# Three of eight stick-breaking heads summed in full fp32 instead of as high and low fp32r parts

## The chip, the cores and the metric

The kernel runs on one core of one Trainium2 chip. The metric is the device time of one execution in microseconds (us); lower is better. Engines are named as the profile names them: PE is TensorE, PEld its weight loads, DVE is VectorE, ACT is ScalarE, POOL is GpSimd, SP is SyncE, which issues most of the DMAs.

## The reference

One layer of a hybrid decoder runs over 512 prompt tokens and 32 sample tokens: a half-step feed-forward block, a mixing block, a second half-step feed-forward block and a per-layer embedding. The mixing block has a gated linear attention (GLA) group of 4 heads and a stick-breaking group of 8 heads. Only the second group is touched here:

```
def sb_attend(q, k, v, q_pos, k_pos, bias):
    z = einsum(q, k) * SB_DH ** -0.5 + bias
    valid = k_pos < q_pos
    log_stay = where(valid, log_sigmoid(-z), 0)
    after = cumsum(log_stay, reverse=True) - log_stay     # over the keys
    w = where(valid, exp(log_sigmoid(z) + after), 0)
    return einsum(w, v)
```

`log_sigmoid(-z)` is minus the softplus of z. So each head needs, for each query, running sums of a softplus over the later keys. All inputs and outputs are fp32.

## The kernel before

Activations are held transposed, features on the 128 partitions and 544 tokens along the row. The large matmuls (feed-forward blocks, projections) are made from three fp32r products, high times high, low times high and high times low; DVE and ACT make the high and low parts. They run before and after the part that matters here.

The stick-breaking heads of the prompt run in a loop over h = 0 to 7. The causal part of a 512x512 score matrix, keys on partitions, is held as 1280 columns: 4 diagonal blocks of 128 (columns 0 to 511), then the blocks right of the diagonal, 384 + 256 + 128 columns. For each head:

1. PE makes the scores of a pair of heads in units (`z_unit`, lines 1014, 1019 and, for the cached pages of the samples, 1030); ACT copies them out with the bias (`logits`, L1619).
2. ACT makes exp and log (`soft_part`, L1629 and L1631), DVE finishes the softplus (`softplus`, L2434) in `sb_s[h % 3]` and signals `sp_ready`.
3. DVE rounds the softplus to fp32r (`high`, L2441 and L2442) and subtracts that from it (`low`, L2447), both parts in fp32r; it signals `sp_low_ready`.
4. PE sums over the keys (`prompt_sums`, L1093): matmuls with a triangular mask within a block and a matrix of ones for whole blocks. There are nine products of 512, 384, 384, 256, 128, 384, 256, 128 and 128 columns, 2560 in all. Each is made twice, of the high and of the low part, so there are 18 matmuls. They go to PSUM banks 4 to 6, of which there is one set, so `prompt_sums(h)` waits for `d_ready` of head h-1.
5. DVE subtracts the sums from the scores (`exponents`, L2454 and L2455) and signals `d_ready`; ACT takes the exponential (`weight`, L1686) and signals `w_ready`.
6. PE multiplies with the values after every second head (`prompt_out`, L1124 and L1126); DVE copies the result out (`pair_out`, L2461).

The order on each engine is written out by hand. PE runs `prompt_sums(h)`, then `prompt_out` of the pair before (h = 2, 4, 6), then the score units that `Z_STEP[h]` names. After h = 5 comes `sample_z` (L1158), after h = 6 `head_sum(0)` and `head_sum(1)` (L1147, sums of squares of the GLA heads, whose squares ACT makes at L1695), and after h = 7 the sample's sums with the full fp32 masks (`sample_sums`, L1168 to L1172), `head_sum` and `prompt_out(3)`. DVE runs for each h: `low(h + 1)`, `exponents(h)`, `softplus(h + 2)`, `high(h + 2)`, and after some heads `pair_out` and copies of the values (L2430).

Of the kernel before, what the change touches and what calls it, by code (L numbers as in the profile page):

```python
# [33 lines left out]
SB_HEADS, SB_DH = 8, 64  # L34
# [83 lines left out]
def build(nc, a, o):  # L118
# [13 lines left out]
    with ctx:  # L132
        def sb(name, shape, dt=F32, where=ctx):
            return where.enter_context(nc.sbuf_tensor(name, shape, dt))

        def sem(name):
            return ctx.enter_context(nc.semaphore(name))

        PS = ctx.enter_context(nc.psum_tensor("PS", [P, 8, 512], F32))
# [9 lines left out]
        ones = sb("ones", [P, P])  # L149
        tri = sb("tri", [P, P])  # L150
# [52 lines left out]
        def scratch(owner, at_, shape):  # L203

            n = 1
            for s_ in shape[1:]:
                n *= s_
            v = owner[0:shape[0], at_:at_ + n]
            if len(shape) == 3:
                return v.rearrange("p (a b) -> p a b", a=shape[1])  # L210
            if len(shape) == 4:
                return v.rearrange("p (a b c) -> p a b c", a=shape[1], b=shape[2])
            return v
# [6 lines left out]
        p_raw = scratch(extra_flat, 8 * HALF, [P, 2, T])  # L220

        spare = [hold_w[:, n, (at["out"][0] + 1) % 2, :] for n in range(2)]
        first_slot, other_slot = at["out"][0] % 2, (at["out"][0] + 1) % 2
        sb_z = [scratch(extra_flat, 0, [P, 1280]), raw[:, first_slot, 0:1280], scratch(spare[0], 0, [P, 1280]),
                scratch(extra_flat, 2560, [P, 1280]), scratch(dead, 2560, [P, 1280]), raw[:, other_slot, 0:1280],
# [2 lines left out]
        sb_s = [scratch(gone, 0, [P, 1280]), scratch(extra_flat, 1280, [P, 1280]), scratch(spare[1], 0, [P, 1280])]  # L228
# [12 lines left out]
        Z_UNITS = [(0, 1, None), (0, 0, None), (0, 2, None), (1, 0, None), (1, 1, None), (1, 2, (0, 0)), (2, 0, None),  # L241
                   (2, 1, (0, 1)), (2, 2, None), (3, 0, None), (3, 1, (1, 0)), (3, 2, (1, 1))]
        Z_FIRST = 5
        TURN = len(Z_UNITS)
        Z_STEP = [(5, 7), (7, 9), (9, 10), (10, 12), (12, 13), (13, 13), (13, 13), (13, 13)]
        PAGE_UNIT = {r: n for n, (p, u, r) in enumerate(Z_UNITS) if r is not None}
# [91 lines left out]
        sig = {n: sem(n) for n in names}  # L338
# [222 lines left out]
        def _(pe):  # L561
            mm = nc.tensor.matmul
# [418 lines left out]
            def z_unit(n):  # L981

                banks_ = unit_banks(n)
                if n in (0, 1, 3):

                    t = T0["rest"] + REST - (3, 2, None, 1)[n]
                    pe.wait_ge(psum_free[t % 2], t // 2 + 1)
                elif n == 4:
                    pe.wait_ge(sig["og_out"], GLA_HEADS)
                    pe.wait_ge(sig["sn_out"], 8)  # L990
                else:
                    pe.wait_ge(sig["z_out"], n if n in (2, TURN) else n - 1)
                if n == TURN:
                    last = pages_turned(banks_[0])
                else:
                    p, u, r = Z_UNITS[n]
                    last = prompt_z(p, u, banks_)
                    if r is not None:
                        last = page_z(*r, banks_[0])
                last.then_inc(sig["z_full"], 1)  # L1000
# [34 lines left out]
            def pages_turned(bank):  # L1035

                for n in range(4):
                    cols_ = slice(n * P, (n + 1) * P)
                    last = nc.tensor.transpose(PS[:, bank, cols_], z_past[:, cols_], ident[:])
                return last  # L1040
# [28 lines left out]
            def natural(r):  # L1069
# [11 lines left out]
                                               flat(proj[:, SV + f])[:, r * P:(r + 1) * P], ident[:])  # L1081
                last.then_inc(sig["nat_full"], 1)

            def prompt_sums(h):

                parts = [sp_low[h % 3][:, a_:b_] for a_, b_ in ((0, 512), (512, 1280))]
                pe.wait_ge(sig["sp_low_ready"], h + 1)
                pe.wait_ge(sig["d_ready"], h)

                def both(out, mask, at_, n, start=False, stop=False):  # L1090
                    for i, (diag, rest) in enumerate((sp_high[h % 2], parts)):
                        src = diag[:, at_:at_ + n] if at_ < 512 else rest[:, at_ - 512:at_ - 512 + n]
                        last = mm(out, mask, src, start=start and i == 0, stop=stop and i == 1)  # L1093
                    return last

                both(PS[:, 4, :], tri_r, 0, 512, start=True, stop=True)
                both(PS[:, 5, 0:384], tri_r, 512, 384, start=True)
                both(PS[:, 5, 0:384], ones_r, 128, 384)
                both(PS[:, 5, 128:384], ones_r, 896, 256)
                both(PS[:, 5, 256:384], ones_r, 1152, 128, stop=True)  # L1100
                if h == 0:
                    pe.wait_ge(sig["nat_out"], 1)
                both(PS[:, 6, 0:384], tri_r, 896, 384, start=True)
                both(PS[:, 6, 0:256], ones_r, 256, 256)
                both(PS[:, 6, 128:256], ones_r, 1152, 128)
                both(PS[:, 6, 256:384], ones_r, 384, 128, stop=True).then_inc(sig["c_full"], 1)
# [46 lines left out]
            def sample_z():  # L1153

                pe.wait_ge(sig["setup_new"], 2)
                pe.wait_ge(sig["z_out"], TURN)
                for p in range(4):
# [16 lines left out]
            for quad in range(2):  # L1174
                pe.wait_ge(psum_free[quad], (T0["merge"] + 1 - quad) // 2)
            for n in range(3, Z_FIRST):
                z_unit(n)
            natural(0)
            for h in range(SB_HEADS):
                prompt_sums(h)  # L1180
                if h == 7:
                    head_sum(2)
                    sample_sums()
                    head_sum(3)
                    prompt_out(3)
                elif h % 2 == 0 and h:
                    prompt_out(h // 2 - 1)
                if h == 6:
                    head_sum(0)
                    head_sum(1)  # L1190
                if h == 1:
                    natural(3)
                for n in range(*Z_STEP[h]):
                    z_unit(n)
                    if n < Z_FIRST + 2:
                        natural(n - Z_FIRST + 1)
                if h == 5:
                    sample_z()
# [93 lines left out]
        def _(act):  # L1292
# [387 lines left out]
            soft_part(1)  # L1680
            for n in range(3, Z_FIRST + 1):
                logits(n)
# [41 lines left out]
            for h in range(SB_HEADS):  # L1724
# [11 lines left out]
                for n in range(*Z_STEP[h]):  # L1736
                    if Z_FIRST < n < TURN:
                        logits(n)
# [127 lines left out]
        def _(dve):  # L1866
# [569 lines left out]
            def high(n):  # L2436
                dve.wait_ge(sig["sp_ready"], n + 1)
                if n >= 2:
                    dve.wait_ge(sig["c_full"], n - 1)
                s_ = sb_s[n % 3]  # L2440
                v.tensor_copy(sp_high[n % 2][0], s_[:, 0:512])  # L2441
                v.tensor_copy(sp_high[n % 2][1], s_[:, 512:1280]).then_inc(sig["sp_high_ready"], 1)  # L2442

            def low(n):
                dve.wait_ge(sig["sp_high_ready"], n + 1)
                for high_, first, end in zip(sp_high[n % 2], (0, 512), (512, 1280)):
                    ins = v.tensor_tensor(sp_low[n % 3][:, first:end], sb_s[n % 3][:, first:end], high_.bitcast(F32),  # L2447
                                          ALU.subtract)
                ins.then_inc(sig["sp_low_ready"], 1)
# [17 lines left out]
            def sample_logits():  # L2467

                dve.wait_ge(sig["setup_new"], 2)
                dve.wait_ge(sig["z_full"], TURN + 1)  # L2470
                v.scalar_tensor_tensor(z_past.rearrange("p (a n) -> p a n", a=2),
                                       PS[:, unit_banks(TURN)[0], :].rearrange("p (a n) -> p a n", a=2), SB_DH ** -0.5,
                                       cols.unsqueeze(1).broadcast_to([P, 2, 256]), ALU.mult,
# [21 lines left out]
            softplus(1, sb_z[1], sb_s[1])  # L2495
            high(1)
            for h in range(SB_HEADS):
                if h + 1 < SB_HEADS:
                    low(h + 1)
                exponents(h)  # L2500
                if h == 0:
                    natural_out(1)
                    natural_out(2)
                elif h == 1:
                    natural_out(3)
                if h + 2 < SB_HEADS:
                    softplus(h + 2, sb_z[h + 2], sb_s[(h + 2) % 3])
                    high(h + 2)
                if h == 5:
                    sample_logits()  # L2510
                elif h == 6:
                    softplus(SB_HEADS, z_past, s_past)
                    softplus(SB_HEADS + 1, z_new, s_new)
                if h % 2 == 0 and h:
                    pair_out(h // 2 - 1)
                if h == 6:
                    out_low(0)
# [63 lines left out]
            n, t, quad, use = F_TILES, *ticket(Step(0), "f2_up0")  # L2581
# [346 lines left out]
```

## Time and profile before

| | |
|---|---|
| median of 3 runs | 1181.87 us (1181.6 to 1182.53) |
| the profiled execution | 1181.77 us, span 1179.6 us |
| PE busy | 1159.6 us, 98% of the span |
| DVE busy | 778.2 us, 66% |
| ACT busy | 547.9 us, 46% |
| granted PE clock | 1.00 |

The profiled execution has a span (first to last instruction) of 1179.6 us; 2.2 us lie around it. The loop over the heads is about 49 us of it, from 602.1 to 651.3 us. PE is almost always busy over the whole span, so the few microseconds where it waits are what other engines can give back. A "duration" in a timeline holds the pipeline's fill and drain: an engine starts the next instruction before the end of the last, and the step from start to start is what a stream of instructions costs.

### The profile page before, as it was taken

Reading aid. Unit: us, or ns where it says so; the run is one execution under the profiler, and the core shown is the slowest. Engines: PE = TensorE matmul, PEld = TensorE weight load, DVE = VectorE, ACT = ScalarE, POOL = GpSimd, SP = SyncE. Lnnn points to the kernel's source line nnn. Section 1 sums busy time; section 2 is a strip of 40 time slices with the busy share of each in tenths; the row PEclk is TensorE's granted clock in tenths of the full one; section 3 lists DMA queues with packets and bytes.
Section 4 is the critical chain, followed back from the end, with each engine's and each line's share of the span. In section 5 each row is a group of like instructions: output and inputs, shape, how many; then the busy total and the mean of one; then the engine's idle time right before and its main releaser. Section 6 shows DMA issues by size and latency. Waiting matters only on the chain.

```text
span 1179.6 us, 23057 instructions
## 1 busy us (share of the span) xinstructions
PE 1159.6 (98%) x9230; PEld 1119.7 (95%) x9230; DVE 778.2 (66%) x1075; ACT 547.9 (46%) x758; POOL 105.3 (9%) x138
## 2 busy tenths in 40 slices
PE   7999999999999999999999999999999999999997
PEld 6999999999999999999877699999999999999996
DVE  6853887368845865655379747863788358864665
ACT  5433555235543532312368745533555225544555
POOL 1600000000002012122050010000000000002102
PEclk9999999999999999999999999999999999999999
DMA  6203331232224032213047151113421233215202
GB/s 220 86 28 124 121 107 54 90 124 93 87 72 148 17 108 73 70 59 113 1 150 241 59 179 37 38 58 93 143 86 68 90 125 107 89 54 179 72 1 77
DMA packets 45405, 110.29 MB, mean 93 GB/s; under 512 B 5458, under 2 KB 11618, under 8 KB 45202
## 3 DMA queue, kind: packets, MB, share of 16 engines
q1 hardware_dynamic: 43522, 103.13, 26.0%
q0 software_dynamic: 1232, 5.01, 1.3%
q8 instruction: 55, 0.90, 0.3%
q10 hardware_dynamic: 576, 1.08, 0.2%
q14 instruction: 20, 0.16, 0.0%
HBM read 103.57 MB, written 5.64 MB: 93 GB/s over the span
## 4 chain that ended last, share of the span: by engine, by line
PE 92%; DVE 4%; ACT 2%; DMA 1%; issue 0%; SPq 0%; DVEq 0%; ACTq 0%
PE PS L584 42%; PE PS L795 29%; PE PS L597 12%; PE PS L915 1%; PE PS L765 1%; DMA raw<-in_f_in 1%; PE PS L618 1%; PE PS L942 1%; PE PS L975 1%; PE PS L978 0%; PE PS L1019 0%; DVE extra L2434 0%; SPq L517 0%; PE PS L1147 0%; DVE w_lo L1874 0%
## 5 line engine op out<-in xcount | busy, mean ns | idle before, releaser
L1300 ACT ACTIVATE w_hi<-raw 128x1024 fp32r<-128x1024 f32 (+2 forms) x77 | 93.2, 1210 | 155.4 <-PE PS L584 128.4
L1874 DVE TENSOR_TENSOR w_lo<-raw,w_hi 128x1024 fp32r<-128x1024 f32 (+2 forms) x76 | 108.1, 1422 | 79.2 <-ACT w_hi L1300 79.2
L795 PE MATMUL PS<-a_lo,w_hi 128*128 128x272 f32 x512 | 148.7, 290 | 0.0
L584 PE MATMUL PS<-a_hi,w_hi 128*128 128x272 f32 x656 | 139.6, 294 | 8.9 <-DVE w_lo L2175 7.6
L795 PE MATMUL PS<-a_hi,w_lo 128*128 128x272 f32 x512 | 147.6, 288 | 0.0
L795 PE MATMUL PS<-a_hi,w_hi 128*128 128x272 f32 x512 | 147.4, 288 | 0.0
L584 PE MATMUL PS<-a_lo,w_hi 128*128 128x272 f32 x656 | 136.3, 289 | 0.0
L584 PE MATMUL PS<-a_hi,w_lo 128*128 128x272 f32 x656 | 136.0, 289 | 0.0
L584 PE MATMUL PS<-h_hi,w_hi 128*128 128x272 f32 x576 | 119.5, 289 | 0.2
L584 PE MATMUL PS<-h_hi,w_lo 128*128 128x272 f32 x576 | 119.2, 288 | 0.0
L584 PE MATMUL PS<-h_lo,w_hi 128*128 128x272 f32 x576 | 118.8, 288 | 0.0
L584 PEld LDWEIGHTS PS<-a_hi,w_hi 128*128 128x128 f32 x656 | 103.2, 189 | 13.5 <-issue 10.7
L584 PEld LDWEIGHTS PS<-a_lo,w_hi 128*128 128x128 f32 x656 | 103.8, 190 | 0.0
L584 PEld LDWEIGHTS PS<-a_hi,w_lo 128*128 128x128 f32 x656 | 103.5, 190 | 0.0
L795 PE MATMUL PS<-b_tail,w_hi 128*128 128x272 f32 x512 | 98.0, 289 | 0.0
L795 PEld LDWEIGHTS PS<-a_hi,w_hi 128*128 128x128 f32 x512 | 96.6, 189 | 0.0
L795 PEld LDWEIGHTS PS<-a_hi,w_lo 128*128 128x128 f32 x512 | 96.4, 188 | 0.0
L795 PEld LDWEIGHTS PS<-a_lo,w_hi 128*128 128x128 f32 x512 | 96.1, 188 | 0.0
L584 PEld LDWEIGHTS PS<-h_hi,w_hi 128*128 128x128 f32 x576 | 90.5, 188 | 0.8 <-DVE h_lo L1995 0.6
L584 PEld LDWEIGHTS PS<-h_lo,w_hi 128*128 128x128 f32 x576 | 90.5, 189 | 0.0
L584 PEld LDWEIGHTS PS<-h_hi,w_lo 128*128 128x128 f32 x576 | 89.9, 189 | 0.0
L795 PEld LDWEIGHTS PS<-b_tail,w_hi 128*128 128x128 f32 x512 | 80.3, 188 | 0.0
(471 smaller groups left out, 2615.6 us busy)
## 6 DMA issues: line engine op xcount, KB each, us to landing
raw<-in_f_in SPq DMA_DIRECT2D x86, 512.0 KB, 4.0
raw<-in_f_out SPq DMA_DIRECT2D x64, 256.0 KB, 2.8
raw<-in_w_rest SPq DMA_DIRECT2D x40, 256.0 KB, 2.8
raw<-in_f_out SPq DMA_DIRECT2D x32, 192.0 KB, 2.4
raw<-in_w_out SPq DMA_DIRECT2D x8, 512.0 KB, 5.0
raw<-in_ple_w_gate SPq DMA_DIRECT2D x8, 512.0 KB, 4.2
x<-in_x SPq DMA_DIRECT2D x8, 272.0 KB, 7.2
raw<-in_w_in SPq DMA_DIRECT2D x4, 512.0 KB, 4.0
```

What stands on the lines that cost most here:

```text
L584: last = mm(PS[0:width, 4 * quad + 2 * c + half, 0:HALF], wt[:, cols], act[:, k, half * HALF:(half + 1) * HALF], start=(k == 0 and n == 0) ...
L597: last = mm(PS[0:width, 4 * quad + 2 * c + half, 0:HALF], wt[:, cols], act[:, k, tok], start=(k == 0 and n == 0), stop=(k == n_k - 1 and n ...
L618: last = mm(PS[:, 4 * quad + 2 + half, 0:HALF], ones[:], squares[:, tok], start=(k < summed), stop=(k == KD - 1))
L765: last = mm(PS[:, 4 * (t % 2) + 2 * c + half, 0:HALF], wt[:, slot, col:col + P], act[:, k, half * HALF:(half + 1) * HALF], start=(k == 0 a ...
L795: last = mm(PS[:, 4 * quad + bank, 0:HALF], w_[:, k * P:(k + 1) * P], a_[:, k, :], start=(start and k == 0 and i == 0), stop=(stop and k = ...
L915: last = mm(PS[:, 2 + hh, tok], k_[r, tok], q_[r, tok], start=True, stop=True)
L942: last = mm(PS[:, 7, n * 256:n * 256 + 256], kl_batch[:, 2 * part + n, :], gv_new[:, p * 256:(p + 1) * 256], start=True, stop=True)
L975: last = mm(PS[:, 2 + hh, tok], gv_nat[:, c, h * P:(h + 1) * P], att[p][:, N_CH * hh + c, :], start=True, stop=(c == 0))
L1300: fn(pair[0][:, 0:width], raw[:, slot, 0:width], ACT.Copy).then_inc(sig["split_hi"], 1)
L1874: v.tensor_tensor(pair[1][:, 0:width], raw[:, slot, 0:width], pair[0][:, 0:width].bitcast(F32), ALU.subtract).then_inc(sig["split_lo"], 1)
```

## The change

A tuple `PLAIN_SUMS = (2, 4, 6)` names the third, fifth and seventh head. For these PE uses `plain_sums`: nine matmuls of fp32 operands, the softplus itself against the fp32 masks `tri` and `ones`, where `prompt_sums` had 18 of fp32r parts. It waits for `sp_ready` instead of `sp_low_ready`. DVE leaves out `high` and `low` for these heads. `split_heads(n)` counts the heads before n that are still split, for the waits on the semaphores of the two parts. Buffers, banks, the masks and the order of everything else stay.

```diff
+        def split_heads(n):
+
+            return n - sum(h < n for h in PLAIN_SUMS)
...
+        PLAIN_SUMS = (2, 4, 6)
...
+            def plain_sums(h):
+
+                s_ = sb_s[h % 3]
+                pe.wait_ge(sig["sp_ready"], h + 1)
+                pe.wait_ge(sig["d_ready"], h)
+                mm(PS[:, 4, :], tri[:], s_[:, 0:512], start=True, stop=True)
+                mm(PS[:, 5, 0:384], tri[:], s_[:, 512:896], start=True, stop=False)
+                mm(PS[:, 5, 0:384], ones[:], s_[:, 128:512], start=False, stop=False)
+                mm(PS[:, 5, 128:384], ones[:], s_[:, 896:1152], start=False, stop=False)
+                mm(PS[:, 5, 256:384], ones[:], s_[:, 1152:1280], start=False, stop=True)
+                mm(PS[:, 6, 0:384], tri[:], s_[:, 896:1280], start=True, stop=False)
+                mm(PS[:, 6, 0:256], ones[:], s_[:, 256:512], start=False, stop=False)
+                mm(PS[:, 6, 128:256], ones[:], s_[:, 1152:1280], start=False, stop=False)
+                mm(PS[:, 6, 256:384], ones[:], s_[:, 384:512], start=False, stop=True).then_inc(sig["c_full"], 1)
+
             def prompt_sums(h):
...
-                pe.wait_ge(sig["sp_low_ready"], h + 1)
+                pe.wait_ge(sig["sp_low_ready"], split_heads(h) + 1)
...
-                prompt_sums(h)
+                (plain_sums if h in PLAIN_SUMS else prompt_sums)(h)
...
             def low(n):
-                dve.wait_ge(sig["sp_high_ready"], n + 1)
+                dve.wait_ge(sig["sp_high_ready"], split_heads(n) + 1)
...
-                if h + 1 < SB_HEADS:
+                if h + 1 < SB_HEADS and h + 1 not in PLAIN_SUMS:
                     low(h + 1)
...
-                    high(h + 2)
+                    if h + 2 not in PLAIN_SUMS:
+                        high(h + 2)
```

PE before, from the end of the score unit ahead of the third head's sums (`proj` holds q and k, `work_r` and `h_hi` the high part, `w_lo` the low part, `sum_r` the masks in fp32r):

```order
L1019 MATMUL PS<-proj 128x256
L1019 MATMUL PS<-proj 128x128 x2
L1093 MATMUL PS<-work_r,sum_r 128x512 [waits d_ready,sp_low_ready]
L1093 MATMUL PS<-w_lo,sum_r 128x512
L1093 MATMUL PS<-h_hi,sum_r 128x384
L1093 MATMUL PS<-w_lo,sum_r 128x384
L1093 MATMUL PS<-work_r,sum_r 128x384
L1093 MATMUL PS<-w_lo,sum_r 128x384
```

PE in the changed kernel, at the same place (`hold_w` is the softplus of the third head):

```order
L1025 MATMUL PS<-proj 128x256
L1025 MATMUL PS<-proj 128x128 x2
L1095 MATMUL PS<-hold_w,tri 128x512 [waits d_ready,sp_ready]
L1096 MATMUL PS<-hold_w,tri 128x384
L1097 MATMUL PS<-hold_w,ones 128x384
L1098 MATMUL PS<-hold_w,ones 128x256
L1099 MATMUL PS<-hold_w,ones 128x128
L1100 MATMUL PS<-hold_w,tri 128x384
L1101 MATMUL PS<-hold_w,ones 128x256
L1102 MATMUL PS<-hold_w,ones 128x128
L1103 MATMUL PS<-hold_w,ones 128x128
```

Nine rows stand where 18 stood. In this listing a matmul of full fp32 is one row; the trace records it as two matmuls.

DVE before, from the third head's softplus to the fourth's (`hold_w` and `proj` are the softplus buffers, `raw` the scores of the second head):

```order
L2434 SCALAR_TENSOR_TENSOR hold_w<-hold_w 128x1280 [waits soft_log]
L2441 CAST work_r<-hold_w 128x512 [waits c_full,sp_ready]
L2442 CAST h_hi<-hold_w 128x768
L2447 TENSOR_TENSOR w_lo<-hold_w,work_r 128x512 [waits sp_high_ready]
L2447 TENSOR_TENSOR w_lo<-hold_w,h_hi 128x768
L2454 TENSOR_TENSOR raw<-raw,PS 128x512 [waits c_full]
L2455 TENSOR_TENSOR raw<-raw,PS 128x768
L2430 COPY v_nat<-PS 128x512 [waits nat_full]
L2434 SCALAR_TENSOR_TENSOR proj<-proj,extra 128x1280 [waits soft_log]
```

DVE in the changed kernel, the same stretch:

```order
L2455 SCALAR_TENSOR_TENSOR hold_w<-hold_w 128x1280 [waits soft_log]
L2475 TENSOR_TENSOR raw<-raw,PS 128x512 [waits c_full]
L2476 TENSOR_TENSOR raw<-raw,PS 128x768
L2451 COPY v_nat<-PS 128x512 [waits nat_full]
L2455 SCALAR_TENSOR_TENSOR proj<-proj,extra 128x1280 [waits soft_log]
```

Four instructions are gone from between the softplus of the third head and the exponents of the second. The same holds one and two pairs of heads later.

## Rows read from the trace of the kernel before

**Rows 1.** The page: one engine's busy time, and the chain by engine.
```profile
PE 1159.6 (98%) x9230; PEld 1119.7 (95%) x9230; DVE 778.2 (66%) x1075; ACT 547.9 (46%) x758; POOL 105.3 (9%) x138
PE 92%; DVE 4%; ACT 2%; DMA 1%; issue 0%; SPq 0%; DVEq 0%; ACTq 0%
```

**Rows 2.** Stretch: length, busy (instructions) of PE, PEld, DVE, ACT, POOL; clock, DMA.
```profile
602.10:651.27 49.17, 45.76 (x459) 38.40 (x458) 45.79 (x63) 41.03 (x55) 7.34 (x13) 1.00 0.61 205
```

**Rows 3.** PE's waits, 602 to 1180 us: total, times, longest.
```profile
PE PS L1093 <- DVE raw L2455: 1.8, 2, 1.3
PE PS L618 <- ACT sq L1360: 1.0, 1, 1.0
PE PS L1080 <- DVE v_nat L2430: 0.9, 1, 0.9
PE PS L1147 <- ACT hold_w L1695: 0.7, 1, 0.7
```

**Rows 4.** Chain of waits, in order of time: start, us, what.
```profile
619.63 1.56 DVE h_hi L2447 x2
...
648.82 2.61 PE PS L1093 x18
```

**Rows 5.** PE's timeline at the third head: start, duration, instruction, idle before.
```profile
615.41 0.92 PE L1019 MATMUL PS<-proj 64*128 64x256 f32 x8
616.81 0.47 PE L1093 MATMUL PS<-work_r,sum_r 128*128 128x512 f32 x1 [0.48 <-DVE raw L2455]
617.12 0.40 PE L1093 MATMUL PS<-w_lo,sum_r 128*128 128x512 f32 x1
...
619.58 0.32 PE L1126 MATMUL PS<-extra,v_nat 128*64 128x128 f32 x1
```

**Rows 6.** PE's timeline, fifth to seventh head: start of sums, what follows them.
```profile
630.19 0.50 PE L1093 MATMUL PS<-work_r,sum_r 128*128 128x512 f32 x1
...
632.99 0.32 PE L1126 MATMUL PS<-hold_w,v_nat 128*64 128x128 f32 x1
...
638.51 1.07 PE L1158 MATMUL PS<-sq,proj 128*32 128x64 f32 x8
640.88 0.47 PE L1093 MATMUL PS<-work_r,sum_r 128*128 128x512 f32 x1 [1.29 <-DVE raw L2455]
...
643.65 0.32 PE L1126 MATMUL PS<-proj,v_nat 128*64 128x128 f32 x1
```

**Rows 7.** PE's timeline where it already multiplies full fp32.
```profile
609.90 0.65 PE L1080 MATMUL PS<-ident,proj 128*128 128x128 f32 x4 [0.93 <-DVE v_nat L2430]
610.31 0.48 PE L1093 MATMUL PS<-work_r,sum_r 128*128 128x512 f32 x1
...
651.27 1.13 PE L1147 MATMUL PS<-hold_w,ones 128*128 128x272 f32 x4
652.24 1.02 PE L1168 MATMUL PS<-extra,tri 128*128 128x512 f32 x2
653.10 0.59 PE L1169 MATMUL PS<-extra,ones 128*128 128x256 f32 x2
653.62 0.69 PE L1170 MATMUL PS<-extra,ones 32*128 32x256 f32 x2
```

**Rows 8.** DVE's timeline: high part, low part and exponents; exponents of the fifth head.
```profile
612.71 0.43 DVE L2441 CAST work_r<-hold_w 128x512 fp32r<-128x512 f32 x1
...
613.64 0.69 DVE L2447 TENSOR_TENSOR w_lo<-hold_w,work_r 128x512 fp32r<-128x512 f32 x1
...
615.12 0.68 DVE L2454 TENSOR_TENSOR raw<-raw,PS 128x512 f32<-128x512 f32 x1
615.72 0.95 DVE L2455 TENSOR_TENSOR raw<-raw,PS 128x768 f32<-128x768 f32 x1
...
633.10 0.69 DVE L2454 TENSOR_TENSOR proj<-proj,PS 128x512 f32<-128x512 f32 x1 [0.56 <-PE PS L1093]
```

**Rows 9.** ACT's timeline: squares of the first two GLA heads.
```profile
645.97 1.19 ACT L1695 ACTIVATE hold_w<-y 128x544 f32<-128x544 f32 x2
```

## The prediction

> **What bounds the kernel now.** I read the page first. PE is busy for 98% of the span and makes 92% of the chain that ended last [rows 1], so a microsecond more of PE work is a microsecond of time unless PE was waiting there. Then the busy time of each engine in the stretch that the change touches, from the first head's sums to the end of the last one's: of 49.17 us PE is busy 45.76 and DVE 45.79, at a granted clock of 1.00 [rows 2]. Neither is far ahead. The chain of waits shows how they share it: for most of the stretch it runs through DVE (high part, low part, exponents, one after the other), and from about 647 us through PE alone [rows 4]. Read alone, this chain would say that DVE is the bound and that relieving it pays in full. PE's own waits say how much that can be worth: in the stretch it waits 1.8 us in two places for DVE's exponents, 0.9 us for a copy of the values and 0.7 us for ACT's squares [rows 3]. These 3.4 us are all that any relief of the other engines can give back there (49.17 - 45.76). None of PE's waits from 602 us on is put down to a DMA; the one behind the stretch that is over 0.7 us, 1.0 us at L618, is for ACT, on work that itself follows PE [rows 3]. So a shift of PE at the end of the heads should go through to the end of the kernel.
>
> **What the change takes from DVE.** The high part takes 0.93 us (612.71 to 613.64) and the low part 1.48 us (613.64 to 615.12) [rows 8], 2.4 us a head and 7.2 us for three heads. That is a sixth of DVE's 45.79 us in the stretch [rows 2], but it lies beside PE's work except where PE waits. DVE's own order also gets shorter between a softplus and the exponents behind it, so the exponents start when the sums are there.
>
> **What it takes from and adds to PE.** The split sums last from 616.81 to 619.58 us in the third head [rows 5], from 630.19 to 632.99 in the fifth and from 640.88 to 643.65 in the seventh [rows 6]: 2.77, 2.80 and 2.77, together 8.34 us. Within them a 128x512 matmul and the first of its partner stand 0.31 us apart [rows 5].
>
> The plain sums are not in the trace, but the same form is: right behind the heads the samples' sums use the fp32 mask `tri`, and their 512 columns are recorded as two matmuls which take 0.86 us, from 652.24 to 653.10 [rows 7]. That is 0.84 ns for a column of one record, 1.68 ns for a column of an fp32 matmul. Narrower ones don't seem to pay a floor: four recorded passes of 128 columns take 0.41 us (609.90 to 610.31), which is 0.80 ns a column, and four of 272 take 0.97 us, or 0.89 ns [rows 7]. So the 2560 columns of a head cost 2560 x 1.68 = 4.30 us. An edge is added: the two records of 256 columns in front of a matmul of other rows take 0.52 us, 0.09 over the rate [rows 7], and behind a head stands such a change too. I take 4.4 us a head, 13.2 us for three. The ends: 4.2 us (the transposes' two times 0.80 ns throughout, 4.1, and the edge) and 5.2 us (the 0.52 us of 256 columns, 2.03 ns a column, throughout). I stay by the row of 512 columns, since it has the same mask, the same operand types and a full set of 128 rows, and the 0.52 us has its edge in it.
>
> PE's work grows by 13.2 - 8.34 = 4.86 us.
>
> On passes the Trainium skill ("FP8 and Floating Point Precision", TensorE Precision Notes) says that true fp32 takes four passes through the array, for the products of high and low halves. Counting passes alone, four stand where two stood, and the sums would double, to 5.56 us a head. The rows say less than double: 0.86 us for 512 columns [rows 7] against 0.31 us for the first of the two split matmuls [rows 5], and for narrow ones hardly more than the pair. What that count would give is a rival below.
>
> **What PE's waits give back.** They are taken one by one.
> - Ahead of the third head PE waits 0.48 us for the second head's exponents [rows 5], which DVE starts at 615.12 [rows 8] only because high and low of the third head stand before them. Without these they start at about 613.2, when the second head's sums end, and are done by 614.8; the score unit ends at 615.41 + 0.92 = 616.33 [rows 5]. All 0.48 us come back.
> - Ahead of the seventh head's sums PE waits 1.29 us for the sixth head's exponents [rows 6]. Here the loop cannot be shorter than exponents behind sums: DVE starts 0.11 us after PE's next operation (633.10 against 632.99) [rows 6, 8], the two subtractions take 1.55 us (615.12 to 616.67) [rows 8], and PE starts 0.14 us later (616.81) [rows 5], 1.80 us in all against 2.37 now (638.51 to 640.88) [rows 6]. So 0.57 us come back, and 0.7 us of waiting stay, which is the wait that takes the place of the old one.
> - Ahead of `head_sum(0)` PE waits 0.7 us for ACT's squares [rows 3], which start at 645.97 [rows 9]. PE comes there about 3.8 us later than now (4.86 - 0.48 - 0.57), and ACT, which follows the sixth exponents, the sample's scores and their softplus, about 3 us later, by 649.0 against PE's 649.8. So 0.71 us come back, with a margin of 0.8.
> - The 0.93 us ahead of the transposes of L1080 [rows 7] lie before the first changed instruction and wait on DVE work that stays. Nothing comes back.
>
> The plain sums of heads 2, 4 and 6 are early enough otherwise: `sp_ready` comes before what `sp_low_ready` needed. The sums of heads 3, 5 and 7 wait for the exponents of a plain head, which now end later; PE has prompt_out and score units between (2 us or more), DVE needs 1.8. Sums: 0.48 + 0.57 + 0.71 = 1.76 us.
>
> **The sum.** +4.86 - 1.76 = +3.10 us on the profiled execution's 1181.77 us is 1184.87; it lies 0.10 under the median of 1181.87, so for a median I say 1185.0 us. A measurement of this kernel tells 0.2%, 2.36 us, from no change, so the line to slower is 1184.2.
>
> **The rivals.**
> - *No change that can be told (under +2.36 us).* The plain sums cost 4.2 us a head: 12.6 - 8.34 - 1.76 = +2.5, and a few tenths more come back, such as the dearer start of the split sums after other matmuls (0.31 against 0.23 us of a 128x512, three times 0.08, [rows 5]). That gives +2.2, 1184.1 us. For it: the narrow passes of L1080. Against: it needs both. Chance 0.17.
> - *Faster: DVE is the bound.* The chain does run through it [rows 4]. If a plain sum cost no more than a split one (the pair of narrow matmuls does cost about what one plain would), 1.76 us would come back and nothing be paid: 1180.1 us. It decides from the point where three plain heads take less than 8.34 + 1.76 = 10.1 us, 3.4 us each. The samples' 0.86 us for 512 columns [rows 7] speak against it. Chance 0.04.
> - *Four passes against two.* 3 x 2.78 = 8.3 us more, less 1.76: +6.6, 1188.5 us. The row of 0.86 us speaks against. Chance 0.04.
> - *Relief hidden anyway.* PE's waits don't shrink because ACT, not DVE, is behind them (softplus of the seventh head, the squares): up to the whole 4.86, 1186.7 us, likelier +3.9 with the squares' 0.7 lost. Chance 0.08.
>
> The forecast keeps 0.67. **Chances:** faster 0.04; same 0.18; slower 0.78, from the forecast, the last two rivals and less a little for its lower edge. The range reaches from 1184.0, into the second case, to 1186.4, where plain heads of 4.85 us end (14.55 - 8.34 - 1.76 = +4.5). The bound of 5.2 us a head (+5.5, 1187.4) and the four passes are left out, with the faster case, as the two in ten.
>
> **What would show it.** In the changed profile, L1095 to L1103 should have 54 matmul records and last about 4.4 us from the first start to the next operation. DVE's busy time in the stretch should be 7 us or so lower and idle time should stand before the exponents, released by PE. PE should have no wait ahead of the third head's sums, 0.7 us ahead of the seventh's, none before L1147 at 650 us. From the last head's sums on, all should be as before, 3.1 us later. The prediction is wrong if a plain head takes under 4.1 or over 4.8 us, if PE shows a new wait for `exponents` ahead of heads 3, 5 or 7, or if the delay at 650 us isn't found again at the end.

## The result

The changed kernel takes 1184.92 us in the median (1182.05 before, in the same rounds), a ratio of 1.0025, 95% interval 1.0018 to 1.0031: 2.1 to 3.7 us slower. Of 18 executions of each kernel one was far off (1213.43 us in the changed kernel, 1613.86 us before); it counts in the median and not in the ratio. The forecast was 1185.0 us. That this is within 0.1 us of the median is partly luck: the difference of the medians is 2.87 us where the forecast had 3.1, and it was added to an earlier median of before (1181.87) that lay 0.18 lower.

The page gives the profiled execution a span of 1183.3 us (1185.45 us with what lies around it); its engine line answers to [rows 1]:

```profile
PE 1165.1 (98%) x9230; PEld 1121.7 (95%) x9230; DVE 772.5 (65%) x1063; ACT 548.6 (46%) x758; POOL 104.1 (9%) x138
```

PE has the same number of records and 5.5 us more to do, DVE 12 instructions and 5.7 us less. The stretch from the first head's sums to the end of the last head's, and from PE's first output matmul (674.22; the window opens 0.02 us ahead of it) to the end, by engine as in [rows 2]:

```profile
602.53:655.02 52.49, 50.83 (x460) 39.54 (x458) 38.88 (x51) 41.73 (x56) 7.33 (x13) 1.00 0.58 192
...
674.20:1183.30 509.10, 501.43 (x3918) 496.42 (x3918) 333.67 (x455) 246.12 (x350) 28.64 (x20) 1.00 0.26 87
```

Before, the same two stretches were 49.17 us [rows 2] and, from the answer to the same view, this:

```profile
670.47:1179.60 509.13, 501.50 (x3918) 496.49 (x3918) 333.90 (x455) 245.86 (x350) 28.62 (x20) 1.00 0.26 87
```

So 3.32 us come in within the stretch, and nothing is made up behind it: its second line is 509.10 us (509.08 from the matmul itself) against 509.13. In the stretch PE is busy 5.07 us longer (50.83 - 45.76) and idle 1.66 us where it had been idle 3.41. DVE is busy 6.9 us less and has nothing to show for it: PE went on setting the pace. The two spans differ by 3.7 us; the rest is 0.43 us ahead of the first head's sums (602.53 against 602.10), where nothing was changed, less the 0.05 behind; in the other profiles of this study that point lies between 601.64 and 602.74, so it belongs to no change.

PE's timeline from the end of the score unit to the products behind the third head's sums, columns as in [rows 5]:

```profile
615.84 0.92 PE L1025 MATMUL PS<-proj 64*128 64x256 f32 x8
616.69 1.12 PE L1095 MATMUL PS<-hold_w,tri 128*128 128x512 f32 x2
617.65 0.81 PE L1096 MATMUL PS<-hold_w,tri 128*128 128x384 f32 x2
618.30 0.81 PE L1097 MATMUL PS<-hold_w,ones 128*128 128x384 f32 x2
618.95 0.59 PE L1098 MATMUL PS<-hold_w,ones 128*128 128x256 f32 x2
619.38 0.38 PE L1099 MATMUL PS<-hold_w,ones 128*128 128x128 f32 x2
...
620.90 0.39 PE L1103 MATMUL PS<-hold_w,ones 128*128 128x128 f32 x2
621.21 0.32 PE L1147 MATMUL PS<-extra,v_nat 128*64 128x128 f32 x1
```

The wait of 0.48 us [rows 5] is gone. From start to start the matmuls of 384, 256 and 128 columns take 0.65, 0.43 and 0.22 us, all about 1.7 ns a column, as the 1.68 of 512 columns, with no floor down to 128. The first takes 0.96 us instead of 0.86 and the last 0.31 instead of 0.22. The head takes 4.52 us, and its nine rows are 18 records, as in the other two plain heads. The fifth takes the same (631.82 to 636.34) and the seventh 4.49:

```profile
641.85 1.07 PE L1179 MATMUL PS<-sq,proj 128*32 128x64 f32 x8
643.66 1.10 PE L1095 MATMUL PS<-proj,tri 128*128 128x512 f32 x2 [0.73 <-DVE raw L2476]
...
648.15 0.32 PE L1147 MATMUL PS<-proj,v_nat 128*64 128x128 f32 x1
...
650.47 2.10 PE L1168 MATMUL PS<-hold_w,ones 128*128 128x272 f32 x8
```

Ahead of the seventh head PE waits 0.73 us (1.29 before, [rows 6]), and none ahead of the squares' sums at 650.47 (0.7 before, [rows 3]). These two are all that is left of PE's waits in the stretch that the profile names, total, times and longest as in [rows 3]; the first lies ahead of the second head and is as it was:

```profile
PE PS L1086 <- DVE v_nat L2451: 0.9, 1, 0.9
PE PS L1095 <- DVE raw L2476: 0.7, 1, 0.7
```

DVE's side of it, its own waits in the stretch:

```profile
DVE extra L2475 <- PE PS L1114: 3.3, 1, 3.3
DVE proj L2475 <- PE PS L1103: 2.8, 1, 2.8
```

These are the two longest. The exponents wait for PE's sums in six of the eight heads now, where it had been two; the time taken from DVE has turned into idle time of DVE.

### The profile page after: what moved, and what is told of

It is laid out like the page before. It is cut to its first block, busy times and chain, and to the rows that moved or that the text cites. A ratio compares the mean times of both kernels' runs of the same rounds, so it can differ in the third digit from the quotient of the medians.

```text
span 1183.3 us, 23042 instructions
## 1 busy us (share of the span) xinstructions
PE 1165.1 (98%) x9230; PEld 1121.7 (95%) x9230; DVE 772.5 (65%) x1063; ACT 548.6 (46%) x758; POOL 104.1 (9%) x138
## 4 chain that ended last, share of the span: by engine, by line
PE 95%; DVE 2%; ACT 1%; issue 0%; DMA 0%; DVEq 0%; ACTq 0%
PE PS L590 43%; PE PS L801 29%; PE PS L603 11%; PE PS L921 1%; PE PS L771 1%; PE PS L1114 1%; PE PS L1025 1%; PE PS L624 1%; PE PS L948 1%; PE PS L981 0%; PE PS L1145 0%; PE PS L984 0%; DMA raw<-in_f_in 0%; PE PS L1168 0%; PE PS L1147 0%
```

## The experiments

Few of these differences can be told apart by the times alone: most intervals are about 1 us to either side. So each experiment is also read in its profile, which is a single execution, from the start of the first head's sums to the start of the first sum of squares (44.65 us before, 602.10 to 646.75; 47.94 in the changed kernel, 602.53 to 650.47).

| kernel | to the first sum of squares | against before | ratio, 95% interval |
|---|---|---|---|
| changed | 47.94 | +3.29 | 1.0025 (1.0018 to 1.0031) |
| e1_parts_kept | 48.80 | +4.15 | 1.0037 (1.0023 to 1.0050) |
| e2_relief_only | 43.58 | -1.07 | 0.9991 (0.9982 to 1.0000) |
| e3_only_seventh | 45.03 | +0.38 | 1.0005 (0.9996 to 1.0014) |
| e4_only_third | 45.63 | +0.98 | 1.0003 (0.9994 to 1.0012) |
| e5_only_fifth | 46.92 | +2.27 | 1.0009 (1.0000 to 1.0018) |
| e6_all_plain | 53.70 | +9.05 | 1.0082 (1.0068 to 1.0095) |
| v2_copy_squares | 43.45 | -1.20 | 0.9994 (0.9985 to 1.0003) |
| v3_squares_first | 45.38 | +0.73 | 0.9997 (0.9988 to 1.0006) |
| v4_copy_squares_pair | 42.99 | -1.66 | 0.9996 (0.9987 to 1.0005) |

**e1_parts_kept: PE's half of the change alone.**

```diff
-            return n - sum(h < n for h in PLAIN_SUMS)
+            return n
...
-                if h + 1 < SB_HEADS and h + 1 not in PLAIN_SUMS:
+                if h + 1 < SB_HEADS:
                     low(h + 1)
...
-                    if h + 2 not in PLAIN_SUMS:
-                        high(h + 2)
+                    high(h + 2)
...
-                    ins = v.tensor_tensor(sp_low[n % 3][:, first:end], sb_s[n % 3][:, first:end], high_.bitcast(F32),
-                                          ALU.subtract)
+                    ins = v.tensor_tensor(high_ if n in PLAIN_SUMS else sp_low[n % 3][:, first:end],
+                                          sb_s[n % 3][:, first:end], high_.bitcast(F32), ALU.subtract)
```

Expected:

> The changed kernel, but DVE still makes high and low part of the third, fifth and seventh head (the low part over the high one, since PE reads neither), 7.2 us of DVE work with no reader. Theory A (PE's plain sums cost 5.2 us, DVE's relief gives back 1.05 us through two waits of PE, and PE coming late covers ACT's squares for 0.7): against before +5.2 - 0.7 = +4.5 us, 1.05 over the changed kernel; PE waits about 0.5 us ahead of the third head's sums and 1.3 ahead of the seventh's, as before, none ahead of the squares' sums. Rival B (relief of DVE is worth nothing, PE's waits vanish because PE comes later): like the changed kernel, +3.3 us. Rival C (DVE's relief is worth its whole length): +3.3 + 7.2 = +10.5 us.

Measured: 1185.85 us, ratio 1.0037 (1.0023 to 1.0050). In its profile PE's waits in the stretch are these:

```profile
PE PS L1095 <- DVE raw L2477: 1.6, 2, 1.1
PE PS L1086 <- DVE v_nat L2451: 0.9, 1, 0.9
```

They are 0.48 us ahead of the third head, as before, and 1.07 ahead of the seventh; the wait for the squares is gone. That is +4.15 us against before and 0.86 over the changed kernel, where theory A had 4.5 and 1.05. The interval of the time, 2.7 to 5.9 us, excludes rival C (7.2 us of DVE work paid in full) but not rival B (+3.3); against B speak the two waits, which are back with DVE as their releaser while the plain sums stay. Of the 0.35 us by which A was off against before, 0.22 are the wait of 1.07 us instead of 1.29. Before, the seventh head's softplus starts on DVE 1.07 us behind the second subtraction ahead of it (633.71 to 634.78), right behind the end of ACT's log (633.48 + 1.27 = 634.75). Here PE, and DVE with it, come later, ACT's log ends at 635.88, and the same step takes 0.87 us (637.04 to 637.91).

**e2_relief_only: DVE's half alone.**

```diff
-                mm(PS[:, 4, :], tri[:], s_[:, 0:512], start=True, stop=True)
...
+                def twice(out, mask, at_, n, start=False, stop=False):
+                    diag, rest = sp_high[0]
+                    for i in range(2):
+                        src = diag[:, at_:at_ + n] if at_ < 512 else rest[:, at_ - 512:at_ - 512 + n]
+                        last = mm(out, mask, src, start=start and i == 0, stop=stop and i == 1)
+                    return last
+
+                twice(PS[:, 4, :], tri_r, 0, 512, start=True, stop=True)
...
```

Expected:

> The other half alone: DVE leaves out high and low part of the three heads and PE waits for the softplus alone, but makes the 18 matmuls of a split sum, in fp32r, reading the first head's high part twice, so the sums of these three heads are left wrong. Theory A: the three heads last 2.8 us each, the 0.48 us ahead of the third head and 0.57 of the 1.29 ahead of the seventh come back, the 0.7 us for ACT's squares stay, since ACT moves along with PE: -1.05 us against before. Rival B: no change. Rival C (the chain of waits through DVE taken at its word): -3 us or more, up to all of PE's 3.4 us of waits in the stretch.

Measured: 1180.48 us, ratio 0.9991 (0.9982 to 1.0000); in the profile -1.07 us, as theory A had it (-1.05). The interval of the time, -2.1 us to none, excludes rival C (-3 us or more) and just reaches rival B (no change); against B speaks the profile. PE's waits in the stretch:

```profile
PE PS L1086 <- DVE v_nat L2459: 0.9, 1, 0.9
PE PS L1100 <- DVE raw L2484: 0.7, 1, 0.7
PE PS L1176 <- ACT hold_w L1724: 0.7, 1, 0.7
```

The wait ahead of the third head is gone, that ahead of the seventh is down to 0.73 us, and the 0.7 us for the squares stay. The three heads' sums take 2.80, 2.81 and 2.76 us, within 0.03 us of before, so nothing else has changed on PE. So 7.2 us of DVE work less are worth 1.07 us to PE. The last of the three waits also settles that the squares' 0.7 us come back in the changed kernel through PE's lateness and not through DVE's relief.

**e3_only_seventh, e4_only_third, e5_only_fifth: one head at a time.**

```diff
-        PLAIN_SUMS = (2, 4, 6)
+        PLAIN_SUMS = (6,)        # e4: (2,)   e5: (4,)
```

Expected:

> Only the seventh head is plain. Theory A: +1.73 for PE's sums (4.5 against 2.77), -0.57 at the wait ahead of it, -0.7 at ACT's squares, which PE now reaches later: +0.45 us against before. If what comes back had nothing to do with the place, it would be a third of the joint change, +1.1 us.

> Only the third head is plain. Theory A: +1.73 us for PE's sums, -0.48 at the wait ahead of them, the later waits stay, since DVE and ACT still make the same work between the fifth head's sums and the seventh's: +1.25 us against before. By thirds of the joint change: +1.1 us.

> Only the fifth head is plain. Theory A: PE did not wait ahead of the fifth head, so DVE's relief there gives back nothing and the whole +1.73 us is paid. By thirds of the joint change: +1.1 us.

Measured, by time: 1181.76, 1182.15 and 1182.75 us, ratios 1.0005 (0.9996 to 1.0014), 1.0003 (0.9994 to 1.0012) and 1.0009 (1.0000 to 1.0018). None is told apart from thirds of the joint change (+1.1 us) by these intervals. The profiles do it: +0.38, +0.98 and +2.27 us. For the seventh head alone PE's waits are 0.9 ahead of the transposes, 0.5 ahead of the third head, 0.7 ahead of the seventh and none for the squares, as forecast, for +0.45. For the third alone they are these:

```profile
PE PS L1114 <- DVE raw L2476: 1.1, 1, 1.1
PE PS L1086 <- DVE v_nat L2451: 0.9, 1, 0.9
PE PS L1168 <- ACT hold_w L1716: 0.7, 1, 0.7
```

That is 0.48 us back ahead of the third head and 0.2 more than forecast ahead of the seventh (1.07 for 1.29, the wait for ACT again): 0.98 instead of 1.25. The fifth head alone comes out 0.5 us above its +1.73, for a reason of its own. The profiled execution is the slowest of e5's eleven (1184.36 us, against a median of 1182.75), and its timeline behind the wait shows why:

```profile
640.61 1.08 PE L1179 MATMUL PS<-sq,proj 128*32 128x64 f32 x8
642.76 0.47 PE L1114 MATMUL PS<-work_r,sum_r 128*128 128x512 f32 x1 [1.07 <-DVE raw L2476]
643.07 1.23 PE L1114 MATMUL PS<-h_hi,sum_r 128*128 128x512 f32 x3
...
647.09 0.32 PE L1147 MATMUL PS<-proj,v_nat 128*64 128x128 f32 x1
```

The seventh head's split sums take 4.33 us, not 2.77. By stretches of 1 us, columns as in [rows 2], with the granted clock third from the end:

```profile
642.00:643.00 1.00, 0.24 (x1) 0.27 (x2) 1.00 (x2) 0.35 (x1) 0.00 (x0) 1.00 1.05 293
643.00:644.00 1.00, 1.00 (x4) 0.85 (x4) 1.00 (x1) 1.00 (x2) 0.00 (x0) 0.55 0.83 268
644.00:645.00 1.00, 1.00 (x5) 1.00 (x5) 0.96 (x4) 1.00 (x1) 0.00 (x0) 0.50 0.86 301
...
647.00:648.00 1.00, 1.00 (x10) 0.58 (x11) 1.00 (x2) 0.97 (x4) 0.00 (x0) 1.00 0.00 0
```

The granted clock is 0.50, the 1.2 GHz level, for about 3.4 us, behind a microsecond in which PE was mostly idle. That costs 1.56 us here and hides the 0.7 us wait for the squares. Without it the sum would be 1.74 for the plain head less 0.22 at the seventh, +1.5 us, with the squares' wait still there. So e5's +2.27 us is no clean measure of the fifth head; its time, +1.1 us (0.0 to +2.1), agrees with this sum and with a third of the joint change alike.

**e6_all_plain: all eight heads.**

```diff
-        PLAIN_SUMS = (2, 4, 6)
+        PLAIN_SUMS = tuple(range(8))
...
-            high(0)
-            low(0)
             natural_out(0)
             softplus(1, sb_z[1], sb_s[1])
-            high(1)
```

`plain_sums` also has the first head's wait for `nat_out` ahead of bank 6, as `prompt_sums` has it.

Expected:

> All eight heads plain, DVE makes no high or low part in this stage. Theory A: 8 x 1.73 = +13.8 us, and all of PE's waits that can come back do, 0.93 + 0.48 + 0.57 + 0.71 = 2.7: +11.1 us against before. Rival B (nothing comes back by relief): +12.4 or more. Rival C (DVE is the bound and 19 us are taken from it): well under +10 us.

Measured: 1191.65 us, ratio 1.0082 (1.0068 to 1.0095), +8.0 to +11.2 us. In the profile +9.05 us to the first sum of squares with seven heads behind it, of which PE's sums make +11.8 (31.2 us against 19.4) and waits -2.7. At the first output matmul it is +10.84 us (681.25 - 602.04 = 79.21, against 68.37), where A had +11.1; the eighth head makes 1.5 of the 1.8 between. The time's upper end excludes rival B (+12.4 us or more); rival C (well under +10) is excluded by the profile alone. The wait of 0.9 us ahead of the transposes has gone too, the one of 0.7 ahead of the seventh head is the last:

```profile
602.04:670.00 67.96, 67.23 (x512) 46.06 (x510) 35.16 (x44) 47.79 (x66) 4.80 (x9) 1.00 0.43 144
```

PE is idle 0.7 us in 68, so in this stretch hardly anything is left to give back, whatever is taken from DVE.

This profile also shows what an edge of the plain sums depends on. The eighth head stands between matmuls of the same form, 128 rows by 128, on both sides:

```profile
657.68 1.02 PE L1095 MATMUL PS<-extra,tri 128*128 128x512 f32 x2
...
662.00 1.08 PE L1170 MATMUL PS<-hold_w,ones 128*128 128x272 f32 x4
```

It takes 4.32 us, the bare rate of 1.68 ns for 2560 columns, and so does the second (4.33), between transposes of that form. The first and the sixth, which have it on one side alone, take 4.42, and the third, fourth and fifth, which have matmuls of fewer rows or columns on both sides, 4.52 or 4.53.

**v2_copy_squares, v3_squares_first, v4_copy_squares_pair: the waits without the plain sums.** The three waits that the change shortened can be attacked by order alone.

```diff
                 if h + 1 < SB_HEADS:
                     low(h + 1)
+                if h == 0:
+                    natural_out(1)
                 exponents(h)
+                if h == 5:              # v4 only
+                    pair_out(1)
                 if h == 0:
-                    natural_out(1)
                     natural_out(2)
...
-                if h % 2 == 0 and h:    # v4 only
+                if h in (2, 6):         # v4 only
                     pair_out(h // 2 - 1)
...
                     log_part(SB_HEADS + 1, z_new, s_new)
+                if h == 5:
                     act.wait_ge(sig["o_full"], 2)
                     head_square(0)
                     head_square(1)
                 weight(h, sb_z[h])
...
                     pe.wait_ge(sig["zs_out"], 1)
+                elif i == 1:
+                    pe.wait_ge(sig["zs_out"], 2)
```

v3 has the last two parts alone, and all are made from the kernel before. Expected:

> The kernel before with two changes of order and nothing plain: DVE copies the second block of values before the first head's exponents, not after, and ACT squares the first two GLA heads before the sixth head's weights, not after the samples' logarithms (PE's second sum of squares then waits for the samples' scores itself). Theory A, that only PE's waits count here: the 0.9 us ahead of the transposes shrink by 0.3 to 0.5, DVE's chain gets 0.45 us shorter, and the 0.7 us ahead of the sums of squares go: -1.2 us against before. If the chain of waits is made up elsewhere: 0 to -0.5 us.

> The kernel before with the squares of the first two GLA heads moved ahead of the sixth head's weights on ACT, alone. Theory A: the 0.7 us ahead of the sums of squares go, 0.7 us less than before. If ACT's other work pays for it (the sixth head's weights start 1.1 us later): the weights are needed only 3 us later by PE, so nothing; should it be otherwise, 0.

> The two changes of order of v2_copy_squares, and DVE copies out the second pair's result after the sixth head's exponents and not ahead of the sixth head's end (0.6 us off DVE's way between the fifth and the sixth exponents). No head is plain. Theory A: the 1.29 us ahead of the seventh head's sums become 0.73, as they did where DVE left out the seventh head's parts; with the 0.8 us that the trace of v2_copy_squares showed at the end of the heads this makes -1.4 us against before. If the wait ahead of the seventh head isn't DVE's length but PE's: -0.8 us, as v2_copy_squares. Where the granted clock of PE falls behind that wait in some executions, a shorter wait should make this rarer, which could take up to 0.5 us more off the median.

Measured: 1181.28, 1181.14 and 1180.81 us, against medians of the kernel before of 1181.61, 1181.64 and 1181.24 in the same rounds; ratios 0.9994 (0.9985 to 1.0003), 0.9997 (0.9988 to 1.0006), 0.9996 (0.9987 to 1.0005). None is shown to be faster by time. In the profiles v2 is 1.20 us earlier at the first sum of squares, as expected, but only 0.80 at the first matmul of the output projection (67.57 us from the first head's sums, 68.37 before). v4 is 1.66 earlier at the first point and 0.57 at the second (67.80). Against expectations of 1.2 and 1.4 us at the end of the heads, v2 fell short and v4 missed; the wait ahead of v4's seventh head was 0.83 us, not 0.73. What v4 gained went into a new wait two steps on:

```profile
644.63 2.10 PE L1149 MATMUL PS<-hold_w,ones 128*128 128x272 f32 x8
...
650.12 1.16 PE L1149 MATMUL PS<-hold_w,ones 128*128 128x272 f32 x4 [0.50 <-ACT hold_w L1697]
```

`head_sum(2)` at 650.12 waits for ACT's next square, which comes behind the seventh head's weights and four logarithms. In v2 this wait is 0.2 us, in the kernel before there is none. v3 was expected 0.7 us earlier and is 0.73 later in its profile, for the same reason as e5: its seventh head's sums take 4.18 us behind a wait of 1.28, with a granted clock of 0.50 from 642 to 645 us. That is 1.41 us more; without it the profile would show the 0.7 us. The last expectation's aside, that a shorter wait makes this rarer and takes half a microsecond off the median, was not borne out by the time. In these rounds none of the kernel before's 15 executions has a mean granted clock under 0.999, so there was little to make rarer; v4's own profile has no such stretch.

## Why the prediction was right

- **PE sets the pace, and DVE's relief pays only where PE waits.** Right. PE's idle time in the stretch fell from 3.41 to 1.66 us, by 1.75, where the forecast had 1.76 from three waits. Each came as it was worked out: 0.48 to nothing, 1.29 to 0.73 and 0.7 to nothing. e2 showed that DVE's half alone is worth 1.07 us, e1 that PE's half alone costs 4.15.
- **The wait that stays.** Right: 0.73 us ahead of the seventh head, against 0.7 forecast, in the changed kernel, e2, e3 and e6 alike. It is the time of the exponents behind the sums, less `sample_z`, and leaving out all of DVE's parts (e6) doesn't shorten it.
- **The cost of a plain head.** The mis-sized term, by a little: 4.52, 4.52 and 4.49 us, 13.53 in all, where I took 4.4 and 13.2. The rate of 1.68 ns a column from the samples' 512 columns was exact. What I undercounted were the edges: I took one of 0.1 us, and there are two, 0.10 us more at the first matmul (0.96 for 0.86 us) and 0.09 behind the last (0.31 for 0.22). Three times 0.1 us is the difference, and e6 shows heads with two, one and no edge at 4.52, 4.42 and 4.32 us. Counting passes would have missed: 4.52 against 2.78 is 1.63 times, not double. A split pair of 128 columns takes 0.23 us (612.77 to 613.00 in the second head before) where a plain matmul of 128 takes 0.22, and at 512 columns two times 0.23 (617.12 to 617.35 before) stand against 0.86.
- **The sum.** +5.19 for PE's sums less 1.75 makes +3.44; the stretch grew by 3.32, against 3.10 forecast. The last 0.12 us is the sum of small steps between heads that I don't take apart.
- **It goes through to the end.** Right: 509.08 us against 509.13 from the first output matmul on.
- **The margin for the squares.** Right in what came of it, but not in its working. I set PE's arrival (649.8) against the start of the squares (649.0), while PE can start only when the first is done: before, that was 0.78 us behind their start (645.97 in [rows 9], PE at 646.75). Counted so, the forecast's own figures had no margin at all. The margin measured is 0.94 us: the squares start at 648.75, so PE could start at 649.53, and it comes at 650.47. Less the 0.43 us of later start, ACT comes 0.68 us earlier than I had it and PE 0.24 later. ACT follows the sixth head's exponents, which have only two plain heads ahead of them and move by 2.34 us (639.19 to 641.96, less 0.43), not by 3. That the mistake did no harm is partly luck. It held beyond the change too: e1, with DVE's parts kept, showed no wait for the squares either.

```profile
648.75 1.19 ACT L1716 ACTIVATE hold_w<-y 128x544 f32<-128x544 f32 x2
```

The rivals fell by the same lines (the +3.9 in the last of them should be +3.8, 4.86 - 0.48 - 0.57): faster needed a plain head under 3.4 us, four passes against two needed 5.6, and relief hidden by ACT needed the waits to stay. The interval of the ratio still reaches down to +2.1 us, so by time alone a difference just under 0.2% isn't excluded; the profile's +3.3 us is what places it.

## What to carry to other kernels

Where an engine is busy for 98% of the span, the most that any relief of the others can pay is the sum of its own waits in that stretch; take these one by one and ask of each what ends it next, before pricing the relief by its own length (7.2 us of DVE work were worth 1.07). A chain of waits that runs through another engine is no measure of what that engine's work is worth. And the form that a change introduces is often already in the trace somewhere: its rate came out exact from one row, while the edges, where the stream changes form, were worth 0.33 us, more than the 0.22 by which the sum was off.

## What was not expected of the hardware

PE's granted clock fell to 0.50 (1.2 GHz) for some 3 us in two of the eleven profiled executions, each time while the seventh head's sums ran: in e5_only_fifth behind a wait of 1.07 us and in v3_squares_first behind one of 1.28. Ahead of the wait stand eight matmuls of 64 columns (`sample_z`), here as in all the kernels. It made 2.77 us of sums into 4.33 and 4.18. The same place with waits of 1.29 us (the kernel before, v2) and 1.07 us (e1, e4) kept the full clock in its profile, and so did all the kernels with 0.73 to 0.83 us there. So the wait's length alone doesn't decide it.

The timed executions say something on how often it happens, since each has its mean granted clock. The two profiled executions with the drop have 0.997 and 0.998, the nine others 0.999 or 1.0. Of the kernels that wait 1.07 us or more there (the kernel before in the rounds of the experiments, e1, e4, e5, v2, v3), 18 of 118 timed executions have 0.998 or less. Of those that wait 0.73 to 0.83 us (the changed kernel, of which 17 executions count here, e2, e3, e6, v4), none of 55 has. In the rounds of e4, e5, e6 and v3 the kernel before took a median of 1182.7 us in the five of its 27 executions with 0.997, and 1181.06 in the fifteen with 1.0. That fits the 1.4 to 1.6 us of a drop. But a mean doesn't say where in an execution the clock fell, the kernel before had none at 0.998 or less among the 15 in v4's rounds and ten among the other 54, and no run varies the wait alone. So that the shorter wait ahead of the seventh head spares the changed kernel these drops fits the counts and is not shown. If it does, the difference of the medians (2.87 us) holds less than the cost of the sums without drops, and the profile's 3.32 is the better measure of that cost.
